# Half of seven tiles' output products moved from the finishing stage into the delta-rule scan

## The reference, cut to what matters

```
m_y = heads_rmsnorm(m_h) * sigmoid(mo) * silu(mz)                  # width 512
r_y = heads_layernorm(r_h + bonus) * silu(rz)                      # width 512
y   = concatenate([m_y, r_y]) @ w_out                              # 1024 x 1024
x   = x + gate * y
```

## Time and profile before

| | us |
|---|---|
| median of 3 runs | 2456.25 (2454.78 to 2457.59) |
| the profiled execution, whole | 2456.63 |
| its span in the trace | 2454.8 |
| scan, batches 6 to 19 (from the key turns of batch 5 to those of batch 19) | 1039.07 to 1301.95 |
| finishing, loop over the tiles up to the last product | 1339.70 to 1506.40 |

### The profile page before, as it was taken

One profiled execution on the slowest core, in us unless ns is written; L12 is line 12 of the kernel. 1 busy time (PEld: TensorE's weight loads), 2 busy tenths in 40 slices (PEclk: granted clock), 3 DMA queues, 4 the chain that ended last, 5 costly groups with the idle time before them and its releaser, 6 DMA issues. The chain is left out here.

```text
span 2454.8 us, 50670 instructions
## 1 busy us (share of the span) xinstructions
PE 2294.7 (93%) x22140; PEld 1417.6 (58%) x22140; DVE 1320.0 (54%) x2181; ACT 794.4 (32%) x1533; POOL 251.0 (10%) x280
## 2 busy tenths in 40 slices
PE   6999999999989988888887998999998999999898
PEld 4444456666644447887784443444685666756443
DVE  3320335553348756777774454555395666667514
ACT  4121222224455653443232222110101445465411
POOL 0000000000002211111221102341100000000000
PEclk8999999999989998999999998999999999999999
DMA  8100122122056654433325422111122100000233
GB/s 332 60 19 7 43 78 76 63 66 73 19 154 145 172 155 112 118 94 95 90 61 196 138 98 76 47 47 34 69 104 80 36 27 27 28 18 10 96 97 117
DMA packets 131866, 207.29 MB, mean 84 GB/s; under 512 B 15629, under 2 KB 95245, under 8 KB 128062
## 3 DMA queue, kind: packets, MB, share of 16 engines
q1 hardware_dynamic: 118398, 154.74, 20.2%
q0 software_dynamic: 13248, 49.32, 7.0%
HBM read 154.01 MB, written 50.01 MB: 83 GB/s over the span
## 5 line engine op out<-in xcount | busy, mean ns | idle before, releaser
L737 PE MATMUL psum<-arena,shared 128*128 128x512 f32 (+1 forms) x864 | 328.3, 524 | 1.5 <-PEq L223 1.5
L2861 PE MATMUL psum<-arena,second_shared 128*128 128x512 f32 (+1 forms) x640 | 282.3, 568 | 11.1 <-PEq L3682 6.4
L737 PEld LDWEIGHTS psum<-arena,shared 128*128 128x128 f32 x864 | 156.9, 191 | 108.5 <-issue 101.5
L2861 PEld LDWEIGHTS psum<-arena,second_shared 128*128 128x128 f32 x640 | 112.4, 195 | 77.0 <-issue 71.8
L1243 PE MATMUL psum<-shared,arena 128*128 128x512 f32 x320 | 150.0, 618 | 0.0
L2247 PE MATMUL psum<-shared,fin_mix 128*128 128x512 f32 x320 | 143.4, 601 | 2.9 <-POOL fin_mix L2380 2.9
L2247 PEld LDWEIGHTS psum<-shared,fin_mix 128*128 128x128 f32 x320 | 59.8, 192 | 75.0 <-issue 71.5
L1243 PEld LDWEIGHTS psum<-shared,arena 128*128 128x128 f32 x320 | 60.3, 196 | 73.3 <-issue 72.9
L841 ACT ACTIVATE shared<-psum 128x512 f32<-128x512 f32 (+1 forms) x48 | 25.2, 525 | 216.2 <-PE psum L737 216.2
L1842 PE MATMUL psum<-r_half,r_lower 64*64 64x32 f32 x3200 | 78.6, 225 | 13.5 <-issue 11.2
L1903 ACT COPY r_half<-psum 128x256 f32<-128x256 f32 x100 | 37.3, 373 | 162.0 <-PE psum L1833 161.7
(11 more groups left out here) (457 smaller groups left out, 4257.6 us busy)
## 6 DMA issues: line engine op xcount, KB each, us to landing
arena<-scratch_operands SPq DMA_DIRECT2D x152, 128.0 KB, 2.7
shared<-in_l_w_in SPq DMA_DIRECT2D x22, 512.0 KB, 4.0
scratch_spill<-shared POOLq DMA_DIRECT2D x16, 640.0 KB, 3.2
second_shared<-in_l_w_in SPq DMA_DIRECT2D x20, 512.0 KB, 3.9
scratch_operands<-arena POOLq DMA_DIRECT2D x14, 640.0 KB, 8.3
scratch_operands<-arena POOLq DMA_DIRECT2D x28, 320.0 KB, 11.3
shared<-in_l_mod_w SPq DMA_DIRECT2D x8, 1024.0 KB, 9.4
t_matrix<-in_transform SPq DMA_DIRECT2D x8, 1024.0 KB, 4.9
```

Source lines behind the costliest of these rows:

```text
L737: last = nc.tensor.matmul(p.psum[:, FILL + f % BANKS, 0:width], weight[:, q % PIECES, k, :], hT[:, k, at:at + width], start=(k == 0), stop ...
L2861: last = nc.tensor.matmul(bank[:, 0:width], w[:, kk, :], hT[:, kk, first:first + width], start=(kk == 0), stop=(kk == KT - 1))
```

## The change

`m_y`'s half of the output products of tiles 3 to 9 is made in the scan. Batches 6 to 19 are 14 units of half a tile's width: four matmuls of 128x512, one in each of four places, into the bank of lane 0's turned keys; ACT copies the sums out, SP stores them to a new scratch `parts`, and finishing loads them and adds them to the other half with one more pass of DVE. The weights of these products are loaded in the scan, in the place of modulation rows 4 and 5, which are loaded at the start of finishing instead. Finishing's start and the places of the gate products are put in another order. With the added semaphores the second clearing falls at the start of `stage_hyena_inputs`, the stage after finishing.

```diff
-    SEMAPHORES_KEPT_FREE = 40
+    SEMAPHORES_KEPT_FREE = 52
...
+PARTS_FIRST_BATCH, PARTS_FIRST_TILE = 6, TILES - (20 - 6) // 2
+LATE_MOD_ROWS = (4, 5)
@@ scan, SP @@
+                        if n == 1 and unit(b) >= 1:
+                            store_part_out(unit(b) - 1)
+                        if n == TOP and ahead and unit(b + 1) >= 0 and unit(b + 1) % 2 == 0:
+                            if unit(b + 1):
+                                sp.wait_ge(parts_ready, unit(b + 1))
+                            load_mix_tile(unit_tile(unit(b + 1)))
@@ scan, PE, turn_keys @@
+                        if lane == 0 and unit(b) >= 0:
+                            pe.wait_ge(parts_copied, unit(b) + 1)
@@ scan, PE @@
+                def part_product(b, k):
+                    u = unit(b)
+                    if u < 0:
+                        return
+                    if k == 0:
+                        pe.wait_ge(keys_copied, 2 * b - 1)
+                        pe.wait_ge(mix_loaded, 16 * (u // 2 + 1))
+                        if u == 0:
+                            pe.wait_ge(out_rows_loaded, 16 * OUT_PARTS)
+                    last = nc.tensor.matmul(bank(KEYS[0]), mix_tile[:, k, :], out_rows[:, k, (u % 2) * BANK:(u % 2 + 1) * BANK],
+                                            start=(k == 0), stop=(k == WT - 1))
+                    if k == WT - 1:
+                        last.then_inc(parts_ready, 1)
...
                     upper_product(b, 2)
+                    part_product(b, 0)
                     if ahead:
                         products(b + 1, 0)
                     half_product(b, 3)
...
                     if before:
                         begin_outputs(b - 1, 1)
                         solve_chunk(b - 1, 1)
+                    part_product(b, 1)
                     half_product(b, 4)
                     if before:
                         update(b - 1, 1)
                         end_outputs(b - 1, 1)
+                    part_product(b, 2)
                     upper_product(b, 4)
+                    part_product(b, 3)
                     if ahead:
                         products(b + 1, 1)
                     half_product(b, 5)
@@ scan, ACT @@
+                def copy_part(b):
+                    u = unit(b)
+                    if u < 0:
+                        return
+                    act.wait_ge(parts_ready, u + 1)
+                    if u:
+                        act.wait_ge(p.parts_stored, 16 * u)
+                    nc.scalar.copy(part_out[:, :], bank(KEYS[0])).then_inc(parts_copied, 1)
...
                     copy_half(b, 4)
+                    copy_part(b)
                     copy_half(b, 5)
@@ finishing, SP, start @@
                 load_bonus(0)
+                load_mix(0)
+                load_bonus(1)
+                load_mix(1)
+                for k in LATE_MOD_ROWS:
+                    sp.dma_start(weights(k), mod_w[:, k, 0:2 * D]).then_inc(sig["mod_loaded"], 16)
@@ finishing, PE @@
                 def first_products(t):
+                    if t >= PARTS_FIRST_TILE:
+                        return
...
                 turn_bonus(0)
-                shift_and_scale()
                 turn_bonus(1)
                 first_products(0)
+                turn_back(0)
+                first_products(1)
+                shift_and_scale()
                 turn_bonus(2)
                 turn_columns()
-                turn_back(0)
                 for i in range(TILES):
                     last_products(i)
                     if i + 1 < TILES:
                         turn_back(i + 1)
                     if i:
                         turn_low(i - 1)
-                    if i + 1 < TILES:
+                    if 2 <= i + 1 < TILES:
                         first_products(i + 1)
                     if i:
                         turn_high(i - 1)
                     if i + 3 < TILES:
                         turn_bonus(i + 3)
-                    if 1 <= i <= 4:
-                        next_gate_products(2 * i - 2)
-                        next_gate_products(2 * i - 1)
+                    if 3 <= i <= 6:
+                        next_gate_products(2 * i - 6)
+                        next_gate_products(2 * i - 5)
@@ finishing, DVE @@
+                        dve.wait_ge(parts_loaded[t % 2], 16 * ((t - PARTS_FIRST_TILE) // 2 + 1))
+                        nc.vector.tensor_tensor(out, products_of_tile, begun[:, t % 2, :], ALU.add).then_inc(sig["gated"], 1)
+                        dve.wait_ge(sig["gated"], t + 1)
+                        then(nc.vector.tensor_tensor(out, out, gate[:, region(t), :], ALU.mult))
```

More of the change, by code:

```diff
@@ L1558, in stage_rwkv_scan @@
     ITEMS = 2 * R_PAIRS
-    PARTS, STORE_PARTS, NEXT_PARTS, V_FIRST, WINDOWS = 4, 4, 8, 10 * C, R_CHUNKS // 2
+    PARTS, STORE_PARTS, OUT_PARTS, NEXT_PARTS, V_FIRST, WINDOWS = 4, 4, 8, 8, 10 * C, R_CHUNKS // 2
+    EARLY_MOD_ROWS = [k for k in range(KT) if k not in LATE_MOD_ROWS]
+    unit = lambda b: b - PARTS_FIRST_BATCH
+    UNITS = B - PARTS_FIRST_BATCH
+    unit_tile = lambda u: PARTS_FIRST_TILE + u // 2
     BEFORE_NEXT = 2 * J + 2 * STORE_PARTS + PARTS
@@ L1667, in load_next_part @@
                         sp.wait_ge(p.last_bonus_stored, 16 * PARTS)
-                    k, e = divmod(n, NEXT_PARTS)
-                    if n == NEXT_PARTS * (KT - 2):
+                    k, e = divmod(n, OUT_PARTS // WT)
+                    rows = slice(e * P * WT // OUT_PARTS, (e + 1) * P * WT // OUT_PARTS)
+                    sp.dma_start(out_rows[rows, k, :], p.dram["l0_w_out"][k * P:(k + 1) * P][rows]).then_inc(out_rows_loaded, 16)
+                def load_next_part(n):
+                    i, e = divmod(n, NEXT_PARTS)
+                    k = EARLY_MOD_ROWS[i]
+                    if k >= KT - 2 and e == 0:
                         sp.wait_ge(v_turned, WINDOWS)
@@ L1717, in _ @@
                     behind()
-                sp.wait_ge(next_loaded, 16 * KT * NEXT_PARTS)
-                for i in range(3):
-                    sp.wait_ge(p.mix_stored[i], 16 * len(range(i, TILES, 3)))
+                store_part_out(UNITS - 1)
+                sp.wait_ge(next_loaded, 16 * len(EARLY_MOD_ROWS) * NEXT_PARTS)
+                sp.wait_ge(p.parts_stored, 16 * UNITS)
             @block.tensor
@@ L2114, in _, with stage_finish @@
                     update_state(B - 1, lane)
-def stage_finish(p, y_chunks, bonus_dram, factor_dram, mix, weights, late, gate_dram, x, x_out, stored, next_gate_dram, hT, weight):
+def stage_finish(p, y_chunks, bonus_dram, factor_dram, mix, weights, late, gate_dram, x, x_out, stored, next_gate_dram, hT, weight, first_weight, parts_dram):
     nc = p.nc
@@ L2137, in stage_finish @@
     bonus_loaded, factor_loaded, mix_loaded, x_loaded = (p.semaphores(f"fin_{n}_loaded", SLOTS) for n in ("bonus", "factor", "mix", "x"))
+    parts_loaded = p.semaphores("fin_parts_loaded", 2)
     gate_weight_loaded = p.semaphores("fin_gate_weight_loaded", GATE_SLOTS)
@@ L2151, in stage_finish @@
         xt = sb("x", [P, SLOTS, D])
+        begun = sb("parts", [P, 2, D])
         sq = sb("squares", [P, 2, W])
@@ L2196, in _ @@
                                  p.dram["mod_b1"][:, g * BANK:(g + 1) * BANK]).then_inc(sig["bias_loaded"], 16)
-                load_bonus(1)
-                load_mix(0)
-                for k in range(WT):
-                    load_weight(k)
                 load_factor(0)
@@ L2204, in _ @@
                     load_weight(k)
+                load_x(0)
+                load_mix(2)
+                for t in range(1, SLOTS):
+                    load_factor(t)
+                    load_x(t)
                 sp.wait_ge(sig["mod_ready"], 1)
                 sp.dma_start(gate, gate_dram).then_inc(sig["gate_loaded"], 16)
-                load_x(0)
-                for t in range(1, SLOTS):
-                    load_mix(t)
-                    load_factor(t)
-                    load_x(t)
+                for t in range(PARTS_FIRST_TILE, PARTS_FIRST_TILE + 2):
+                    load_begun(t)
                 for t in range(SLOTS, TILES):
@@ L2254, in first_products @@
                         pe.wait_ge(sig["gated"], t - 1)
-                    products(t, range(WT))
+                    products(t, range(WT)).then_inc(sig["first_ready"], 1)
                 def last_products(t):
                     pe.wait_ge(sig["mixed"], t + 1)
+                    if t >= PARTS_FIRST_TILE:
+                        pe.wait_ge(sig["gated"], t - 1)
                     products(t, range(WT, KT)).then_inc(sig["products_ready"], 1)
@@ L2391, in _ @@
                 multiply(0)
-                pool.wait_ge(sig["mod_ready"], 1)
-                for k in range(GATE_SLOTS):
-                    load_gate_weight(k)
                 for i in range(TILES):
@@ L2398, in _ @@
                     store(i)
-                    if i in (2, 3):
-                        load_gate_weight(2 * i)
```

(9 more changed lines are left out.)

68 lines of the change are left out of this document (49 added, 19 removed).

## The result

The changed kernel takes 2475.56 us (median of 4 runs, 2472.95 to 2477.51) against 2456.92 us of the kernel before on the same chip: **a ratio of 1.0077, 95% interval 1.0059 to 1.0094**, slower. Measured again later, it gave 1.0074 (1.0050 to 1.0097). The forecast was 2469.7 us, a ratio of 1.0053, in a range of 2446 to 2486. The time lies in the range and on the side given, 5.9 us above the number.

The account below looks back on a forecast made before the run. PE was taken as the bound: busy throughout finishing's loop, idle 34.0 us in scan batches 6 to 19. Scan +30.9 and finishing -17.8 (clock's +8.5 included) put +13.1 on the profiled 2456.6: 2469.7 us, range 2446 to 2486.

Parts of the forecast that it names:

- The scan's +30.9: Scan batches 6 to 19: added matmuls +49.5, refunds -8.3, -9.0 and -1.3, together +30.9 us.
- 56 matmuls ... 0.88 each: Scan: 14 batches x 4 added matmuls of 128x512 at 0.88 us each, +49.5 us.
- a block without one keeps its pause: Scan: issue pauses shrink only in instruction blocks with an added matmul, -9.0 us; 22 us between half 5 and upper 2 stay.
- The refund at `update`: Scan, before half 4: ACT's copy runs beside the added matmul, so 12 pauses x 0.69 us go, -8.3 us.
- The weight loads on SP keep their total: Scan, SP's loads: 2 MB replace 2 MB, so they were put at no cost.
- The pause before `turn_high`: Finishing's loop, i = 2 to 8: PE waits 2.64 us each for ACT's `copy_low`, +18.5 us.
- six of eight: Finishing: the clock falls at three in four of eight pauses, 1.7 us each, +10.2; less the old 1.7, +8.5 us.
- the old 1.7 us: Finishing, last(0): 8.83 instead of 7.13 us at the low clock behind the old pause; counted as going away.
- Pauses refunded wherever they stand: Rival, scan: only the total of instruction pauses counts, so the scan costs +7; 2446 us, chance 0.17.
- No refund at all: Rival, scan: the four places are no gaps, the matmuls push the chain, scan +49.5; 2488 us, chance 0.10.
- The clock stays up: Rival, finishing: no pause lowers the clock, 10.2 us less; 2459.5 us, chance 0.13.
- It falls at all eight: Rival, finishing: every one of the eight pauses is followed by the low clock; 2473 us, chance 0.10.

Follow-up runs that it names:

- spread: Changed kernel with a part's four matmuls spread evenly: before half 2, after upper 2, before half 4, before pull; 2463.15 us, ratio 1.0035.
- block: Changed kernel with all four matmuls of a part in a row before half 4, none elsewhere; 2481.07 us, ratio 1.0110.
- one place: Changed kernel with only the part matmul before half 4 kept, the other three left out; 2454.75 us, ratio 1.0003.
- dummies: Changed kernel with two unused 128x512 matmuls in each pause before `turn_high` (i = 2 to 8), order unchanged; 2461.81 us, ratio 1.0028.

## Why the prediction was right, and where it was not

PE's pauses in scan batches 6 to 19, each counted in PE's timeline from the start of the matmul before it to the start of the one behind it, so that no modelled end hides any, and the time that the granted clock stood at 1.2 GHz (all in us):

| kernel | length | "issue", half 5 to upper 2 | "issue", upper 2 to half 5 | waits for ACT, DVE, DMA | at 1.2 GHz |
|---|---|---|---|---|---|
| before | 262.9 | 24.4 | 9.0 | 10.5 | 10.2 |
| changed | 294.2 | 16.1 | 0.8 | 0.4 | 3.4 |
| changed, again | 290.3 | 13.9 | 1.6 | 0.4 | 0 |
| spread | 284.8 | 3.6 | 0 | 3.1 | 6.8 |
| block | 299.1 | 24.1 | 3.1 | 2.8 | 10.2 |
| one place | 274.7 | 25.5 | 4.6 | 2.4 | 23.9 |

- **The sign and its cause held.** The scan costs more than finishing gives back, because PE's idle time in a scan batch was mostly instruction pauses, which are refunded by place and not from a common store, and because `first_products` was the cover of the chain through ACT's `copy_low`. The same work took 284.8 to 287.3 us in the spread order (three executions), 290.3 to 294.2 in the changed kernel's order (four) and 299.1 as a block (one).
- **The scan's +30.9 was right by two errors that cancel.** "56 matmuls ... 0.88 each" took the duration from a row of such matmuls in a stream; alone among small ones one takes 1.06 us, so the term is 59.4, not 49.5. The refunds were too small by as much: 59.4 - 31.3 = 28.1 us came back, against 18.6. By the table 26.6 of them are pauses: 7.7 of ACT's (8.3 forecast), 2.4 of DVE's (1.3), 8.2 of "issue" between upper 2 and half 5 (9.0), and 8.3 of "issue" between half 5 and upper 2, for which I had nothing. So the step that was off is "a block without one keeps its pause": 22 us were to stay in that stretch, 16.1 and 13.9 did. Which of the four matmuls shortened them was not tried; the four before half 4 did not (24.1). The last 1.5 us was not placed; the clock, which stood low for 6.8 us less, can be a part of it. The refund at `update` held, in the changed kernel and alone.
- **"The weight loads on SP keep their total" is a step that failed.** The total stayed, the rate did not: 256 KB parts in the slots of 128 KB parts doubled it in batches 4 and 5. That cost 2.0 us in batch 5 and some 1.5 in batch 6 (22.6 us against 21.1 in the next), and more in the spread order. I had looked only for who waits for a transfer's data. The kept traces show that the instruction packet itself is late. In the three executions with 128 KB loads the packet that ends the pause near 1025 starts 1.5 us after PE has entered the block before (254 instructions earlier) and takes 0.9 to 1.2 us; in the nine with 256 KB it starts after 2.0 to 2.7 us and takes 1.3 to 1.4. In between the DMA engines are busy for 0.43 to 0.58 of the time there, and for 0.81 to 0.88 here. In all twelve PE goes on 1.3 to 1.5 us after the packet has landed.
- **Finishing's loop: -26.2 forecast with the moved 7.1, -25.3 measured.** The pause before `turn_high` was 2.41 to 2.53 us against 2.64, last(1)'s 2.02 against 2.0, the columns' 1.96 against 2.0, bonus(1)'s 0.95 as forecast.
- **The clock** was a matter of odds and stays one: six of eight were taken, five and seven were found in two executions of one kernel. What I missed is that the pauses at the start count as well. First(0), behind the bonus turns, took 9.17 us instead of 7.13, and last(0), behind the columns' pause, 8.73: the old 1.7 us was not refunded, it only found another pause. Together that is 3.6 us. The whole distance between the forecast's sum and the execution's is 3.2 (16.3 - 13.1), but other parts of it cancel, such as the early batches' +2.7 and the tail's -2.7, so that the closeness of the total is in part luck.
- **The tail**: the way from the last product to the next stage grew by 2.3 us, 1.2 for DVE's second pass and 1.0 for the semaphores' clearing (an idle 1.35 us of DVE where there were 0.32); the stages after it gained 3.7 us, of which the clearing that left them may explain a part. Why they differ was not tried.
- **The rivals.** Pauses refunded wherever they stand: refuted by the block, though the changed kernel did get back 8.3 us in the stretch where 13 would have turned the sign. No refund at all: wrong for the four places and for one. The clock stays up: did not happen, but dummies that make it so are worth 6.6 us. It falls at all eight: did not happen either, though seven of eight came near.

The Trainium skill, "TensorE: Matmul & The Clock Gate", section "HAM oscillation", describes waits that bring the low clock back in every tile; the traces agree for five and for seven of eight pauses, not for all. The Trainium skill, "Runtime: NRT & Kernel Launch", section "Instruction fetch mechanics", calls the crossing of a block mostly hidden; here a dense stream of small matmuls spent 25.8 of 262.9 us in such pauses, and the measurement decides.

## What to carry to other kernels

Idle time of an engine can be filled only where it stands: before work is moved into "gaps", split the idle time by cause and place. Before a stretch of one execution is held against a forecast, look at its granted clock: 24 us at 1.2 GHz went with a stretch that showed a refund of 3 us where the pauses had shrunk by 11.4. Take out of a loop only what covers no chain, or put something else into the cover in the same edit; here the order of a few calls decided between +0.7% and -0.1%, and what then came late was a transfer behind two others in one queue. Look at the rate of the transfers that replace others, not only at their sum.

## What the chip showed that I had not expected

- A lone 128x512 fp32 matmul among 64x32 and 64x64 ones costs 1.06 us of PE's stream, four in a row 0.91 each.
- Transfers of 256 KB instead of 128 KB in the same slots lengthened an instruction pause from 0.75 us (1.02 in one execution) to between 1.57 and 2.12 us in the same place of the stream, because the instruction packet started later and took longer.
- Of equal pauses of 2.4 to 2.5 us some are followed by the 1.2 GHz clock and some are not, in one execution and from one to the next: the products' span of one kernel was 168.8 and 171.9 us.
